# A two-layer hybrid decoder step on one core: convolution taps read straight from PSUM, the feed-forward input normalised ahead of its products, and small products alternated between the two row halves

## What is computed

```python
def mixer_layer(x, pos, attn, hg_state, conv_prev, g, w_in_l, w_out_l, lb, norm_g, cw):
    h = rmsnorm(x, g) @ w_in_l
    ...                                             # q, k, v, hq, hf, hi, hg, cb, cc, ch
    a = attn(q, k, v)                               # 8 query heads, 4 key heads, width 64
    o_h, S = hgrn2_mixer(hq, hf, hi, hg, lb, norm_g, hg_state)   # 4 heads, per-head rmsnorm
    yc, conv_new = causal_dwconv(cc * ch, conv_prev, cw)
    y = jnp.concatenate([a, o_h, cb * yc], axis=-1) @ w_out_l
    return x + y, ...

def cross_attn(x, g, wq, wo, mk, mv):               # 4 heads, 256 memory tokens
    ...

def causal_dwconv(u, prev, w):                      # width 3
    full = jnp.concatenate([prev, u], axis=1)
    y = full[:, 0:T] * w[0] + full[:, 1:T + 1] * w[1] + full[:, 2:T + 2] * w[2]
    return y, full[:, T:]

def conv_ffn(x, g, w_up_l, cw, w_down_l, prev):     # D_FF = 2816
    u = rmsnorm(x, g) @ w_up_l
    u, new = causal_dwconv(u, prev, cw)
    a, b = jnp.split(u, 2, axis=-1)
    return (jax.nn.silu(a) * b) @ w_down_l, new
```

## Time and profile before

| | before |
|---|---|
| median of 3 runs | 983.64 us (983.27 to 990.16) |
| the profiled execution | 979.36 us, of which its span (first to last instruction) 977.7 us |
| PE busy | 883.2 us (90%) |
| DVE / ACT / POOL busy | 680.2 / 439.2 / 455.2 us (70 / 45 / 47%) |
| mean clock granted to PE | 0.966 |
| layer 0: mixer and `out`, to about | 211 us |
| layer 0: cross attention; `xo`; `up`; `down`, to about | 244.6; 254.4; 423.7; 495.7 us |
| layer 1: mixer and `out`, to about | 681 us |
| layer 1: cross attention; `xo`; `up`; `down`, to about | 715.4; 725.5; 894.9; 966.5 us |

### The profile page before, as it was taken

How to read it: one execution, slowest core, us unless ns; L and a number is a source line. 1 busy time by engine, 2 the same in 40 slices (tenths; PEclk the granted TensorE clock), 3 DMA queues, 4 the chain that set the end, 5 groups by cost and what they waited for, 6 DMA issues and landing times.

```text
span 977.7 us, 17665 instructions
## 1 busy us (share of the span) xinstructions
PE 883.2 (90%) x6466; PEld 812.4 (83%) x6466; DVE 680.2 (70%) x1250; ACT 439.2 (45%) x740; POOL 455.2 (47%) x689
## 2 busy tenths in 40 slices
PE   5889999796898888899989999999879888889996
PEld 4889988784798888889989998788559888888996
DVE  4567863754589999985556886376366999999533
ACT  4452552527454445443444254243474445443432
POOL 1312310523557777766741231043154777776761
PEclk9989999998799999999999999989779999999999
DMA  8744531567164455446547552138714455444442
GB/s 250 189 126 141 171 85 44 160 178 205 47 169 130 133 157 142 130 134 199 156 133 183 164 169 87 44 114 224 206 44 130 130 142 156 134 130 139 153 141 65
DMA packets 209408, 137.71 MB, mean 141 GB/s; under 512 B 23476, under 2 KB 202204, under 8 KB 209324
## 3 DMA queue, kind: packets, MB, share of 16 engines
q1 hardware_dynamic: 199904, 111.11, 40.4%
q0 software_dynamic: 8288, 22.85, 8.1%
q10 hardware_dynamic: 1131, 2.64, 0.8%
HBM read 131.13 MB, written 5.44 MB: 140 GB/s over the span
## 4 chain that ended last, share of the span: by engine, by line
PE 50%; POOL 17%; issue 13%; ACT 10%; DVE 5%; DMA 3%; POOLq 1%; DVEq 1%; ACTq 0%; SPq 0%
PE banks L1233 12%; PE banks L1234 11%; PE banks L1235 11%; POOL ring_r L870 10%; ACT keysT_r L1119 3%; ACT vals_r L1119 3%; POOL phase L904 3%; PE banks L1425 2%; POOL phase L897 2%; PE banks L1228 2%; DMA rawk<-in_cache_mem_k 1%; POOL phase L905 1%; PE banks L1343 1%; DMA ring<-in_w_in 1%; PE banks L1518 1%
## 5 line engine op out<-in xcount | busy, mean ns | idle before, releaser
L1235 PE MATMUL banks<-mix_r,ring_r 128*128 128x288 f32 x1008 | 301.4, 299 | 0.0
L1921 DVE SCALAR_TENSOR_TENSOR phase<-phase,fpar 128x304 f32<-128x304 f32 x176 | 198.9, 1170 | 3.7 <-ACT phase L1171 0.4
L1235 PEld LDWEIGHTS banks<-mix_r,ring_r 128*128 128x128 f32 x1008 | 194.5, 193 | 0.0
L1233 PE MATMUL banks<-mix_r,ring_r 128*128 128x288 f32 x480 | 150.8, 314 | 14.5 <-issue 8.9
L870 POOL TENSOR_TENSOR ring_r<-ring,keysT_r 128x1024 fp32r<-128x1024 f32 (+2 forms) x36 | 98.6, 2738 | 40.2 <-ACT keysT_r L1119 36.3
L1234 PE MATMUL banks<-XG_r,keysT_r 128*128 128x288 f32 x384 | 115.2, 300 | 0.0
L1233 PEld LDWEIGHTS banks<-mix_r,ring_r 128*128 128x128 f32 x480 | 93.7, 195 | 21.1 <-issue 17.4
L1119 ACT CAST ring_r<-ring 128x1024 fp32r<-128x1024 f32 x60 | 62.5, 1046 | 101.2 <-DMA ring<-in_w_in 75.1
L1234 PE MATMUL banks<-XG_r,ring_r 128*128 128x288 f32 x352 | 106.8, 303 | 0.0
L1233 PE MATMUL banks<-mix_r,keysT_r 128*128 128x288 f32 x288 | 89.1, 309 | 18.7 <-POOL ring_r L870 16.8
L1235 PE MATMUL banks<-phase_r,ring_r 128*128 128x288 f32 x352 | 103.1, 293 | 0.0
(11 more groups left out here) (296 smaller groups left out, 2201.2 us busy)
## 6 DMA issues: line engine op xcount, KB each, us to landing
ring<-in_w_up SPq DMA_DIRECT2D x88, 512.0 KB, 5.2
ring<-in_w_in SPq DMA_DIRECT2D x36, 512.0 KB, 4.0
ring<-in_w_down SPq DMA_DIRECT2D x16, 1024.0 KB, 5.4
ring<-in_w_down SPq DMA_DIRECT2D x8, 768.0 KB, 4.8
rawk<-in_cache_k POOLq DMA_DIRECT2D x32, 128.0 KB, 2.8
vals<-in_cache_v POOLq DMA_DIRECT2D x32, 128.0 KB, 2.4
ring<-in_w_in SPq DMA_DIRECT2D x16, 256.0 KB, 3.9
rawk<-in_cache_mem_k POOLq DMA_DIRECT2D x16, 256.0 KB, 5.5
```

The source lines that it names most:

```text
L1233: mm(out_, hi_w, hi_x, start=start, stop=False)
L1235: return mm(out_, lo_w, hi_x, start=False, stop=stop)
L1921: last = v.scalar_tensor_tensor(out=y[ab][:, 0:304], in0=uab[i % 2][ab][:, w:304 + w], scalar=fpar[:, 3 * l + w, c:c + 1], in1=y[ab][:, 0: ...
```

## The change

**Feed-forward entry.** The input of `up` is normalised before its products: after `xo` the sum of squares (now with the squares on ACT, L1073 of after, into a ring of four tiles) and its inverse root come first, then a new step `up_split`: DVE multiplies each tile of `X` by gain and `Rn` and puts the sample columns in order of step, latest first; ACT casts; DVE subtracts. The first two `up` pieces (four banks) are multiplied together, contraction tile by contraction tile.

**Up loop.** Nothing is multiplied by `Rn` any more. ACT takes the tap of the present step from the bank (L1155), writes the 16 columns of state behind the 288 of the bank (L1156) and copies the last two steps out (L1157). DVE adds the other two taps reading the bank itself, a prompt part and a 32-column sample part for each. POOL's pads and copies and its subtraction for the input go; its share of an `up` weight piece falls from four tiles to two (`LO_DVE["up"]` 4 to 6). Silu, gate and cast are on 288 columns, and the gate of i follows in iteration i, where it was in i + 1.

**Normalisation.** ACT makes the first value straight from the bank, with scale and bias in the activation; DVE refines with three instructions where it had one and four.

**Row halves.** `level`, `diag`, `diag_s`, `cross` and `as` are issued for both heads together, a matmul of one half and then of the other, into two banks; `ao`, `ho`, `hstate` and `xov` alternate their output halves in one bank. `mv` multiplies 256 columns at once where it had two times 128. The sample states are stored in other pieces (one more store for each of the four groups), and the `down` residual adds the sample columns apart.

```diff
-LO_DVE = {"in": 8, "out": 8, "up": 4, "down": 3}
+LO_DVE = {"in": 8, "out": 8, "up": 6, "down": 3}
...
     for m in range(8):
         a("D", "xo", m)
-    a("op", "pads", 0)
+    a("D", "ssq", 2)
+    a("op", "up_split")
     a("op", "rest", "up", 2, l)
     for i in range(FT):
         ahead = ("up", i + 2) if i + 2 < FT else ("down", i + 2 - FT)
+        a("D", "up", i, 0)
         if i:
             a("op", "round", *ahead, l)
-        a("D", "up", i, 0)
-        if i:
-            a("op", "convolve", i - 1)
+            a("op", "rest", *ahead, l)
+        a("op", "silu", i)
         a("D", "up", i, 1)
-        if i + 1 < FT:
-            a("op", "pads", i + 1)
-        if i:
-            a("op", "gate", i - 1)
-            a("op", "rest", *ahead, l)
-        if i == 0:
-            a("D", "ssq", 2)
-    a("op", "convolve", FT - 1)
-    a("op", "gate", FT - 1)
+        a("op", "gate", i)
...
+                ac(vv[:], bank(l, step, arg)[:, 0:N], ACT.Abs_reciprocal_sqrt, bias=eps,
+                   scale=1.0 / width).then_inc(s["rms_guess"], 1)
...
+                elif step == "up_split":
+                    pe_done(act, l, "turn_cmem", 7)
+                    for k in range(KT_D):
+                        act.wait_ge(s["xn"], KT_D * l + k + 1)
+                        nc.scalar.copy(xg_hi[k], XG[:, k]).then_inc(s["xg_hi"], 1)
...
-                    ac(yab[i % 2][ab][:, 0:304], uab[i % 2][ab][:, 0:304], ACT.Identity,
-                       scale=fpar[:, 3 * l, c:c + 1]).then_inc(s["u_c0"], 1)
+                    ac(yab[i % 2][ab], b_[:, 0:N], ACT.Identity, scale=fpar[:, 3 * l + 2, c:c + 1])
+                    nc.scalar.copy(b_[:, N:N + 16], ust[:, j, g])
+                    nc.scalar.copy(ulast[:, j, g], b_[:, SEQ - 2:SEQ + 16]).then_inc(s["u_y"], 1)
...
-                    r = slice(64 * i, 64 * i + 64)
-                    for t in (0, 1, 2) if m < DEC_SEQ else (0, 1):
-                        for p in (0, 1):
-                            n, c = (P, slice(P * t, P * t + P)) if t < 2 else (NS, slice(SEQ, N))
-                            at = 64 * (2 * t + p) if t < 2 else 256 + NS // 2 * p
+                    pair = (ps[:, (fill - 1) % 8, :], o)
+                    tiles = [(t, p) for t in ((0, 1, 2) if m < DEC_SEQ else (0, 1)) for p in (0, 1)]
+                    for t, p in tiles:
+                        n, c = (P, slice(P * t, P * t + P)) if t < 2 else (NS, slice(SEQ, N))
+                        at = 64 * (2 * t + p) if t < 2 else 256 + NS // 2 * p
+                        for i in (0, 1):
+                            r = slice(64 * i, 64 * i + 64)
                             q = hq[r, p, c].rearrange("p (n two m) -> p n two m", two=2, m=m)[:, :, 1]
-                            last = mm(o[0:n, at:at + n // 2], hk[r, p, c], q, start=True, stop=True)
+                            last = mm(pair[i][0:n, at:at + n // 2], hk[r, p, c], q, start=True, stop=True)
...
+                elif step == "up" and args[0] < 2:
+                    if args != (0, 0):
+                        continue
+                    for n in (5, 6, 7):
+                        pe.wait_ge(emptied[banks.before[fill - n][0]], banks.before[fill - n][1])
+                    first = [parts_of(l, "up", i) for i in (0, 1)]
+                    for k in range(KT_D):
+                        pe.wait_ge(s["xg_lo"], KT_D * (2 * l + 1) + k + 1)
+                        for n in range(4):
+                            hi_w, lo_w = first[n // 2]
+                            c = slice(P * (n % 2), P * (n % 2) + P)
+                            last = split_product(ps[:, (fill + n) % 8, 0:N], hi_w[:, k, c], lo_w[:, k, c], xg_hi[k], xg_lo[:, k],
+                                                 k == 0, k == KT_D - 1)
...
             def rms(l, step, arg, width):
-                b_ = put(l, step, arg)
-                drain()
-                v.tensor_scalar(vv[:], b_[:, 0:N], 1.0 / width, EPS, ALU.mult, ALU.add).then_inc(emptied["D"], 1)
+
+                b_ = bank(l, step, arg)
                 guesses[0] += 1
                 dve.wait_ge(s["rms_guess"], guesses[0])
-                newton(Rn[:], vv[:], sqr[:])
+                drain()
+                v.scalar_tensor_tensor(out=sqr[:], in0=b_[:, 0:N], scalar=width * EPS, in1=vv[:], op0=ALU.add,
+                                       op1=ALU.mult).then_inc(emptied["D"], 1)
...
+                        tap = fpar[:, 3 * l + w, c:c + 1]
+                        d = 2 - w
+                        v.scalar_tensor_tensor(out=y[:, d:SEQ], in0=b_[:, 0:SEQ - d], scalar=tap, in1=y[:, d:SEQ],
+                                               op0=ALU.mult, op1=ALU.add)
+                        last = v.scalar_tensor_tensor(out=y[:, SEQ:N], in0=b_[:, SEQ + 8 * d:N + 8 * d], scalar=tap, in1=y[:, SEQ:N],
+                                                      op0=ALU.mult, op1=ALU.add)
```

More of the change, by code:

```diff
@@ L385, in emptied_order @@
         if step[1] == "ssq" and step[0] < DEPTH:
-            while out[at - 1][1] in ("in", "xq", "up", "round", "pads"):
+            while out[at - 1][1] in ("in", "xq", "round"):
                 at -= 1
@@ L1032, in _ @@
                     j0, j1 = ((0, 8), (8, UJ))[args[0]]
[L1033 to L1034 removed]
+                    src = bank(l, step, *args)[:, 0:64 * (j1 - j0)].rearrange("p (j b w) -> p j b w", b=8, w=2)
+                    for w in (0, 1):
+                        dst = ust[:, j0:j1].rearrange("p j g (w b) -> p (j g) w b", w=2)[:, :, 1 - w]
+                        last = take(l, step, args, dst, src[:, :, :, w])
+                    last.then_inc(emptied["A"], 1)
                 elif step == "as":
@@ L1329, in _ @@
                     t = args[0]
-                    for c in (0, 1):
-                        w = whole(l, P_MV + c)
-                        for k in range(KT_D):
-                            last = mm(o[:, P * c:P * c + P], mg[:, k, P * t:P * t + P], w[:, k], start=k == 0, stop=k == KT_D - 1)
+                    whole(l, P_MV)
+                    whole(l, P_MV + 1)
+                    q = P_MV % 4
+                    w = ring[:, 2:4].rearrange("p s (h k c) -> p (s h) k c", h=2, c=P)[:, q:q + 2]
+                    for k in range(KT_D):
+                        last = mm(o[:, 0:256], mg[:, k, P * t:P * t + P], w[:, :, k], start=k == 0, stop=k == KT_D - 1)
                 elif step == "turn_mk":
@@ L1407, in _ @@
                 elif step in ("diag", "diag_s"):
-                    i = args[0]
+                    if args[0] == 0:
+                        continue
                     pe.wait_ge(s["gates_ready"], l + 1)
-                    r = slice(64 * i, 64 * i + 64)
-                    for t in (0, 1) if step == "diag" else (2,):
-                        for p in (0, 1):
-                            n, c = (P, slice(P * t, P * t + P)) if t < 2 else (NS, slice(SEQ, N))
-                            at = P * (2 * t + p) if t < 2 else NS * p
-                            last = mm(o[0:n, at:at + n], hk[r, p, c], hq[r, p, c], start=True, stop=True)
+                    pair = (ps[:, (fill - 1) % 8, :], o)
@@ new lines, in _ @@
+                    tiles = [(t, p) for t in ((0, 1) if step == "diag" else (2,)) for p in (0, 1)]
+                    for t, p in tiles:
+                        n, c = (P, slice(P * t, P * t + P)) if t < 2 else (NS, slice(SEQ, N))
+                        at = P * (2 * t + p) if t < 2 else NS * p
+                        for i in (0, 1):
+                            r = slice(64 * i, 64 * i + 64)
+                            last = mm(pair[i][0:n, at:at + n], hk[r, p, c], hq[r, p, c], start=True, stop=True)
+                            if (t, p) == tiles[-1]:
+                                last.then_inc(filled, 1)
@@ new lines, in _ @@
+                    c = FT * ab + i
+                    dve.wait_ge(s["u_y"], 2 * FT * l + 2 * i + ab + 1)
+                    b_ = bank(l, step, i, ab)
+                    y = yab[i % 2][ab]
+                    for w in (1, 0):
+                        if w == 0:
+                            drain()
+                        tap = fpar[:, 3 * l + w, c:c + 1]
[4 more added lines that the diff above has]
+                                                      op0=ALU.mult, op1=ALU.add)
```

242 lines of the change are left out of this document (133 added, 109 removed).

## The result

The change makes the kernel faster: 925.31 us in the median of 4 runs (923.13 to 937.14) against 984.03 (983.27 to 990.16). One run of the change, 937.14, has a lower clock than the others (0.950 against 0.963 to 0.969); without it its median is 924.24 and the ratio 0.938, with an interval of 0.933 to 0.943.

A forecast was written before the change was run, and what follows sets the result against it. PE bounds the mixers; in the up loop it waits for POOL's weight subtraction. Feed-forward -23.2 and mixers -20 give -43 from 979.36, so 936; with 4.3 for the median of runs, 940 us, range 925 to 963.

The forecast's parts named there:

- The sign: Whole kernel: faster by over 1% (under 974 us), chance 0.88.
- Ring: Up loop: a cycle through ACT and DVE sets a period of 6.5 us an iteration, 18.0 us less a layer.
- Rival 3: Up loop: POOL subtracts ahead of DVE and holds it, period 7.74 to 8.3, whole 986 to 1007 us; chance 0.10.
- Rivals 2 and 4: Up loop: 2, ring longer, period 7.0, 959 us, chance 0.14; 4, still POOL-bound, period 7.48, 976 us, chance 0.02.
- Taps from PSUM: Up loop: DVE reading PSUM costs nothing extra, 0.44 us for 288 columns against 0.46 from SBUF.
- The entry: Feed-forward entry: up(3) starts 33.5 us after `xo` instead of 27.1, so 6.4 us more a layer.
- PE's start: Feed-forward entry: PE waits about 7.7 us behind `xo` until the input is normalised.
- the gap ahead of up(3): Feed-forward entry: up(3) waits for weights until 10.1 us after the first pieces, where up(2) ends at +6.4.
- The slow start: Feed-forward entry: after the idle gap PE runs at 1.2 GHz instead of 2.4, costing 2.75 us.
- The mixers' work: Mixers: `level` pairs 4.1 us less a layer, `ho` 4.0, `diag` and `ao` together 1.
- the gap ahead of `out`: Mixers: a shorter normalisation chain, 2.3 us instead of 2.88, brings the gap from 3.15 to 2.
- Rival 1: Mixers: the halves don't overlap more, 9 to 13 us of gain are lost, 951 us; chance 0.14.

The follow-up runs named there:

- experiment 8: The change plus extra matmuls with unused results while PE waits at the feed-forward entry and ahead of up(3): 926.63 us, ratio 0.945.
- Experiment 4: The change with the weights of up(3) split before the loop instead of in iteration 1: 923.67 us, ratio 0.941.
- experiment 2: The change without its row halves, all eight products issued as before: 949.63 us, ratio 0.968.
- second trace of before: The kernel before run once more, unaltered: median 978.78 us, ratio 0.999; its profiled execution took 987.7 us.
- second of after: The changed kernel run once more, unaltered: 923.63 us, ratio 0.940; its profiled execution has a loss by the clock of 20.2 us.
- 9: The change with `level` alone issued in its old order, one head in full and then the other: 936.53 us.
- 10: The change with `ho` alone issued in its old order: 941.22 us.
- experiment 6: The change with POOL's share of an `up` weight piece back at four tiles of eight: 935.83 us, ratio 0.953.

## Why the prediction was wrong

**The sign and the places were right.** The up loop, the entry, the mixers, in this order of size, and a clear gain.

**The loop: right.** Ring 6.49 forecast, 6.44 measured, each start within 0.08; 19 iterations and the turn 124.1 forecast, 123.6 and 124.4 measured. Rival 3 had the lever right (the order of DVE and POOL), and DVE does go first. Rivals 2 and 4 are out with it. Taps from PSUM cost nothing more than from SBUF: 0.48 for 255 columns, and 0.53 for 304 less 49 columns at 1.06 ns is 0.48 too. The 65 ns more that the Trainium skill, "VectorE: DVE Perf Modes", section on the TRN2 errata, would give an instruction from PSUM are not there; the measurement decides. One price was wrong: the taps of 32 columns take 0.24, not the 0.18 of the earlier trace rows, whose row is of another kind of instruction; that the b half's taps still take 1.44 (1.425 forecast) is luck, since successive records overlap by about as much.

**The entry: 1.5 too dear**, +4.9 in place of +6.4 in both layers. PE's start, 7.96 behind `xo` (forecast 7.7, though its pieces add to 7.6), and the gap ahead of up(3), 3.40 (3.7), are as forecast. The slow start cost about 1.4 there (the time that experiment 8 saves; in the trace of the change some 12 products stand 0.24 apart in place of 0.133, at a granted clock of 0.51), where I had taken 2.75 from the start of the run. And one reading was wrong though its number was right: I took the gap ahead of up(3) for a cost to be saved. Experiment 4 shows that it is hidden behind the ring.

**The mixers' work: right in sum.** `level` 5.0 a layer (4.1), `ho` 4.1 (4.0), `ao` 1.1 and `diag` 0.5 (1 together), the gap ahead of `out` 1.05 less in layer 0. Rival 1 is out by experiment 2. By layers the sum does not come out: 9.3 and 16.9 measured, 9.5 and 10.5 forecast; with the loss by the clock taken off, which rose from 9.3 to 14.1 in layer 0 and fell from 14.7 to 4.8 in layer 1, it is 14.1 and 7.0.

**The step that failed is the clock.** I priced only the slow start behind the idle gap that the change adds, 2.75 a layer and so +5.5, and put the rest of the run's clock at no change, without a reason. Set against the spans less the loss by the clock, the sum of the other terms holds: before 977.7 - 29.2 = 948.5; after 924.5 - 26.3 = 898.2 and 920.8 - 20.2 = 900.6; a difference of 48 to 50 (46 to 49 with the second trace of before, 986.0 - 39.1 = 946.9), where the forecast without its 5.5 has 48.5. What remains is clock: not +5.5, but -3 between the two first profiled executions and -9 to the second of after. This is a sum to within a few us and no more, since not all of the loss is on the path. The other 5 us of the miss are in the choice of execution: I added 4.3 for the median of three runs of before, and the change's profiled execution lies 1.1 above its median. The gain of clock lies in layer 1 between `in` and `xo`, where before lost 14.7 us and after 4.8. Experiments 2, 9 and 10 show that the order of the row halves is part of the reason; in the first trace of before it is 3.4 of those 14.7, behind `ho`. The rest stands behind waits of PE, and why there are fewer such stretches after the change stays open.

**The range** followed from the wrong sign of that term: its lower end, 925, allowed 15 us below the forecast for engines that overlap more and a warm start at the entry, and nothing for a clock that recovers elsewhere.

## What to carry to other kernels

Where matmuls use half of the array's rows or columns, issue the two halves in turn: here that took 50% off `level` 1 (2.52 to 1.27 us) and `ho`, 32% off the `level` pairs of 16 records (1.53 to 1.04) and 25% off `ao` (1.07 to 0.81), and the clock behind `level` stayed up. A gap of the busiest engine is worth its length only if the chain that feeds it has slack: measure the feeding ring from start to start before repairing the gap, since 6.45 behind 6.40 hid 3.4 us. And count the slow-clock stretches of the kernel before as a term of their own, spread over several executions: a change to what PE does moves them too, in either direction.

## What the runs showed that was not expected

- The clock fell with PE busy throughout: behind the unpaired `level` products to 0.79 to 0.83 over 8 us, and not behind the paired ones.
- DVE and POOL, released by the same event, start 0.13 to 0.14 apart, DVE first, for 39 of the 42 `up` weight pieces in the trace of the change (0.45 to 0.55 for the other three); that is enough to decide who holds whom for 1.76 us.
- A DVE instruction held by POOL had 0.32 of its 0.46 us left when POOL ended (experiment 6), so not the whole instruction is put off. The earlier trace rows had shown it: the DVE instruction there ends at 447.34, 0.31 behind POOL's 447.03, where the prediction read that it ends as POOL does.
- Repairs did not add: 2.0 and 6.5 us apart, 18.0 together; the clock was higher with both, and why isn't shown.
